# Two-layer decoder step on one core: prompt attention's denominators spread by matmuls from their columns, and the row turns of the q, k, v projections behind the next part's first tile

## The chip, the cores and the metric

The kernel runs on one core of one Trainium2 chip. The metric is the device time of one execution in microseconds (us). The engines are TensorE (PE; its weight loads are listed as PEld), VectorE (DVE), ScalarE (ACT), GpSimd (POOL) and SyncE (SP), whose queue issues nearly all of this kernel's DMAs. Each works through its own instructions in order and waits for the others by semaphores.

## What is computed

The reference is one inference step of a decoder trunk of two layers over 512 prompt tokens and 8 sample tokens (each with a past of 4096), model width 1024. The kernel holds both kinds as columns 0 to 519 of one transposed activation (samples first). Cut to what matters here:

```python
# layer 0: multi-head latent attention, 16 heads; prompt part
s = (q_nope @ k_nope + q_pe @ k_pe) * scale          # per head, causal
p = softmax(s)                                        # rows of 128 queries
o = p @ v                                             # then @ w_o, residual, MLP
# layer 1: dilated attention, 3 groups (window, dilation) = (128,1), (512,4), (2048,16), 8 heads of 64
qkv = (x @ w_qkv).reshape(B, S, 3, 3, 8, 64)          # q, k, v of each group
# prompt: per group scores, exp, values; merged by denominators
# sample: keys and values of the stored state plus the new k, v
# returned too: for each group the last rows of k and v (prompt) and the updated state (sample)
# then @ w_o, residual, MLP, final norm
```

Every output of the reference is stored: the two activations, the latents, and the k and v rows of the dilated groups.

## The kernel before

All large matrix products are made by `linear` and `whole`: a weight chunk of 8 x 128 rows by 256 columns (1 MB) is loaded by SyncE into one of two slots (`chunk`), ScalarE rounds it into a high part (L1936), GpSimd subtracts to get the low part (L2281), and TensorE makes three products for each 128 x 128 weight tile and each half of 260 columns (L529, L530, L533). One output tile of 128 rows by 520 columns takes 48 matmuls into one of four PSUM units of two banks each; `z_begin` lets TensorE write a unit when all but the last three units before it have been taken (`tile_taken`), and `z_end` counts `tile_summed`. SyncE may load chunk n when the split of chunk n-2 is done (`chunk_low`).

**Prompt attention** goes over 16 heads in pairs and four query tiles of 128 for each pair: step n is pair p = n // 4, tile t = n % 4. TensorE's step holds, in this order: `scores(n)` (L738), at t = 2 `values(p-1)` (L779) and `spread_den(p-1)` (L767), `turn(n-2, 0)` (L753), one projection of the next pair for t < 3 (`project`, L529 to L533 for q, L706 to L708 for k), at t = 3 `latent_queries` (L718), `turn(n-2, 1)`, and at t = 1 `turn_den(p-1)` (L760). The turns are transposes of the exponentials, one per key block, into PSUM bank 4 or 5; ScalarE copies them out (`keep`, L2044 and L2047). The list `turn_order` numbers everything that goes through banks 4 and 5, and all waits on `turned_ready` and `turned_taken` are counted by it. VectorE masks the scores and takes their maximum (L1546 to L1548), ScalarE exponentiates and sums (`probs`, L2031).

The division by the softmax denominators is put off to the output. VectorE takes the reciprocals of eight columns (L1551: two heads by four query tiles). `turn_den` turns them to eight rows, ScalarE copies these (`rdenT`, L2078), `spread_den` multiplies them with a table `pick8` into bank 4, so that each half of 64 rows holds the reciprocals of its head over 512 columns, ScalarE copies that (`shareP`, L2067), and VectorE multiplies the output with it (L1561). The output goes on to ScalarE (`hA`, L2083) and GpSimd. The last pair has no projection beside it (n < 28 only), nor do the steps behind it.

**The q, k, v projections of layer 1** go over nine parts `QKV` (q of the three groups, then k, then v), each with four output tiles in two weight chunks; tiles are numbered 0 to 35. VectorE takes each tile with a multiplication (L1775) into `dq`, `dk` or, for v, the scratch `tmp` (and copies the samples' columns into `vS`, L1778). At the end of a part TensorE waits until all its tiles are taken and turns them to rows by `to_rows` (L936, four transposes a unit): one unit for the eight samples, one more per kept tile of k (one for group 0, four for groups 1 and 2), four for v. VectorE copies a unit out (`row_tile`, L1690), k and samples into `nat`, a buffer of two slots, each free again when its store has landed (`nat_stored`), v into `dv`. SyncE's `store_part` waits for each row unit and stores it (L1238); for part p-1 it stands behind both chunks of part p in SyncE's queue.

Spread over the same tiles is the attention of the samples (`sample_step`): behind tiles 8 to 11, 13 to 16 and 18 to 21 VectorE scores two of the 24 (group, sample) key blocks each, a product (L1705) and a sum (L1707) for each; their keys (`load_keys`, L1271) and queries (`load_queries`, L1279, the stored q rows spread to 128 partitions) are loaded by SyncE. Behind tiles 24 to 28 come new scores (L948; VectorE L1718 to L1733), maxima and sums (L955, L959, L963), and behind tiles 28, 30, 32, 34 the values of two samples each (L972), whose value rows SyncE loads by `load_values` (L1286) into eight buffers; L980 behind tiles 29, 31, 33, 35 sums them. In SyncE's queue the first eight value loads stand at part 7 behind `store_part` of part 6; loads 14 to 19 and 20 to 23 follow the two chunks of the output projection, which stand behind `store_part` of part 7.

## Time and profile before

| what | value |
|---|---|
| three runs | 1597.49, 1596.48, 1589.59 us; median 1596.48 |
| profiled execution | 1591.77 us, its span 1589.9 us |
| mean granted TensorE clock | 0.970 of 2.4 GHz |
| TensorE's matmuls | busy 1471.6 us, 93% of the span |
| prompt attention | 102 to 262 us |
| q, k, v projections | 850 to 1091 us |
| ScalarE copy and GpSimd split of a weight chunk | L1936 1486 ns and L2281 3541 ns, means over 127 |
| ScalarE exponential (L2031) | 525 ns mean over 64 |
| value and key rows from the state, 256 KB | 5.8 us median from issue to landing |

The profile is of one execution. A row of the chain gives the start, the length, the engine, the tile or line, and how many instructions it merges; a row of a timeline adds the operation, the shapes, and in square brackets how long the engine had been idle before it and what ended that. Matmuls of 32-bit operands leave two records each. The page's clock line for 40 slices of 39.7 us reads 9969996999899999999999999999979999999999, in tenths of full speed.

### The profile page before, as it was taken

To read this page: it belongs to the slowest core of one execution; us is meant where nothing else is said; L and a number is where in the kernel's file an instruction comes from. 1 tells how busy PE (TensorE), PEld (TensorE's weight loads), DVE (VectorE), ACT (ScalarE), POOL (GpSimd) and SP (SyncE) were. 2 spreads that over 40 slices of the span, in tenths; PEclk is the share of its full clock that TensorE was granted. 3 is DMA by queue.
4 is the path that set the end of the run, shared out by engine and by line. 5 is a ranking of instruction groups with operands and counts; after the bars stand their busy time and mean duration, and the time that the engine had idled before them with its cause. 6 is when DMAs were issued, how large, how long until landed. Compare 5 with 4: busy or idle time off the path is not lost.

```text
span 1589.9 us, 28142 instructions
## 1 busy us (share of the span) xinstructions
PE 1471.6 (93%) x12047; PEld 1356.4 (85%) x12047; DVE 686.2 (43%) x984; ACT 470.2 (30%) x882; POOL 613.0 (39%) x276
## 2 busy tenths in 40 slices
PE   6969996788999999999999999998879999999997
PEld 6857763455799999999999999887669999999997
DVE  4667775787245410143113456324567330034212
ACT  4215554333332211122321111113633221122222
POOL 2412222343245644466343434222014654356441
PEclk9969996999899999999999999999979999999999
DMA  4234753776234543453433465556932543533421
GB/s 156 75 100 160 245 183 121 274 295 239 87 134 159 185 159 132 139 202 137 158 140 124 135 233 186 168 198 212 324 126 71 195 150 141 209 135 132 159 80 54
DMA packets 124075, 258.80 MB, mean 163 GB/s; under 512 B 7265, under 2 KB 104689, under 8 KB 117713
## 3 DMA queue, kind: packets, MB, share of 16 engines
q1 hardware_dynamic: 117840, 219.75, 40.1%
q0 software_dynamic: 6144, 37.75, 6.4%
q8 instruction: 68, 1.11, 0.3%
q14 instruction: 23, 0.18, 0.0%
HBM read 249.88 MB, written 95.58 MB: 217 GB/s over the span
## 4 chain that ended last, share of the span: by engine, by line
PE 83%; DVE 9%; issue 3%; ACT 2%; DMA 2%; SPq 1%; another core or an unknown queue 0%; POOL 0%; DVEq 0%; ACTq 0%
PE ps L529 22%; PE ps L533 22%; PE ps L530 21%; PE ps L830 4%; PE ps L738 2%; PE ps L851 1%; ACT sc L2229 1%; PE ps L779 1%; PE ps L753 1%; DVE KT L1536 1%; PE ps L1021 1%; PE ps L1055 1%; DVE sq L1705 1%; PE ps L718 1%; PE ps L871 1%
## 5 line engine op out<-in xcount | busy, mean ns | idle before, releaser
L2281 POOL TENSOR_TENSOR whl<-wraw,whl 128x2048 fp32r<-128x2048 f32 (+3 forms) x127 | 448.6, 3541 | 554.6 <-ACT whl L1936 554.6
L529 PE MATMUL ps<-hA,whl 128*128 128x260 f32 x1216 | 323.2, 287 | 11.6 <-POOL hA L2281 6.0
L530 PE MATMUL ps<-hA,whl 128*128 128x260 f32 x1216 | 318.4, 283 | 0.0
L1936 ACT ACTIVATE whl<-wraw 128x2048 fp32r<-128x2048 f32 (+3 forms) x127 | 186.1, 1486 | 437.3 <-PE ps L533 379.4
L529 PE MATMUL ps<-uT,whl 128*128 128x260 f32 x1024 | 268.4, 283 | 0.0
L530 PE MATMUL ps<-uT,whl 128*128 128x260 f32 x1024 | 266.3, 281 | 0.0
L533 PE MATMUL ps<-hA,whl 128*128 128x260 f32 x1216 | 247.2, 285 | 0.0
L529 PEld LDWEIGHTS ps<-hA,whl 128*128 128x128 f32 x1216 | 231.1, 190 | 16.6 <-issue 15.2
L530 PEld LDWEIGHTS ps<-hA,whl 128*128 128x128 f32 x1216 | 231.8, 191 | 0.1
L533 PE MATMUL ps<-uT,whl 128*128 128x260 f32 x1024 | 206.8, 283 | 0.0
L530 PEld LDWEIGHTS ps<-uT,whl 128*128 128x128 f32 x1024 | 193.2, 189 | 0.0
L529 PEld LDWEIGHTS ps<-uT,whl 128*128 128x128 f32 x1024 | 192.6, 188 | 0.0
L533 PEld LDWEIGHTS ps<-hA,whl 128*128 128x128 f32 x1216 | 187.9, 190 | 0.0
L1649 DVE TENSOR_TENSOR xT<-xT,ps 128x520 f32<-128x520 f32 (+1 forms) x48 | 33.4, 696 | 351.9 <-PE ps L533 341.2
L529 PE MATMUL ps<-hB,whl 128*128 128x260 f32 x640 | 168.3, 284 | 0.0
L530 PE MATMUL ps<-hB,whl 128*128 128x260 f32 x640 | 166.8, 282 | 0.0
L533 PEld LDWEIGHTS ps<-uT,whl 128*128 128x128 f32 x1024 | 156.7, 188 | 0.0
L2281 POOL TENSOR_TENSOR uT<-tmp,uT 128x520 f32 x64 | 84.3, 1318 | 132.2 <-ACT uT L1946 132.2
L1668 DVE SCALAR_TENSOR_TENSOR tmp<-ps,rstd 128x520 f32<-128x520 f32 x64 | 44.8, 700 | 200.3 <-PE ps L533 199.7
L533 PE MATMUL ps<-hB,whl 128*128 128x260 f32 x640 | 129.0, 283 | 0.0
L530 PEld LDWEIGHTS ps<-hB,whl 128*128 128x128 f32 x640 | 120.7, 189 | 0.1
L529 PEld LDWEIGHTS ps<-hB,whl 128*128 128x128 f32 x640 | 120.4, 188 | 0.1
(299 smaller groups left out, 2019.5 us busy)
## 6 DMA issues: line engine op xcount, KB each, us to landing
out_ds<-in_state SPq DMA_DIRECT2D x32, 2047.0 KB, 10.2
wraw<-in_w_up SPq DMA_DIRECT2D x32, 1024.0 KB, 5.6
wraw<-in_w_down SPq DMA_DIRECT2D x32, 1024.0 KB, 5.1
wraw<-in_w_qkv SPq DMA_DIRECT2D x18, 1024.0 KB, 5.6
out_ds<-in_state SPq DMA_DIRECT2D x8, 2044.0 KB, 12.5
dv<-in_state SPq DMA_DIRECT2D x36, 256.0 KB, 5.8
dv<-q_scratch SPq DMA_DIRECT2D x6, 1024.0 KB, 7.2
wraw<-in_w_omla SPq DMA_DIRECT2D x4, 1024.0 KB, 12.3
```

What stands on the lines that cost most here:

```text
L529: pe.matmul(ps[:, 2 * u + a, 0:HALF], hi(k), rhs(k, 0)[:, c], start=first, stop=False)
L530: pe.matmul(ps[:, 2 * u + a, 0:HALF], hi(k), rhs(k, 1)[:, c], start=False, stop=False)
L533: ins = pe.matmul(ps[:, 2 * u + a, 0:HALF], lo(k), rhs(k, 0)[:, c], start=False, stop=last)
L718: ins = pe.matmul(ps[:, 6 + k, LQ + h * NS:LQ + (h + 1) * NS], wuk_pair(p)[:, a, k * P:(k + 1) * P], qS[0:NOPE, h, :], start=True, stop=Tr ...
L738: ins = pe.matmul(ps[:, 2 * (n % 2) + a, 0:(t + 1) * P], qh[:, h % 4, tok], kh[:, h % 4, 0:(t + 1) * P], start=True, stop=True)
L753: ins = pe.transpose(ps[:, bank, b * P:(b + 1) * P], pr[:, n % 3, a, b * P:(b + 1) * P], ident[:])
L779: ins = pe.matmul(ps[a * VD:(a + 1) * VD, 5, b * P:], v[:, b, h * VD:(h + 1) * VD], turned(a, b, 1, slice(b * P, NP)), start=(b == 0), sto ...
L830: ins = pe.matmul(ps[64 * g:64 * g + 64, k, 0:UC], qbd[b % 2][:, j, :, :].rearrange("p q h -> p (q h)"), moving, start=(j == 0), stop=(j = ...
L1649: free(dve.tensor_tensor(cols(xT, f), cols(xT, f), zt(u), ALU.add))
L1668: free(dve.scalar_tensor_tensor(out=out, in0=zt(u), scalar=0.0, in1=rooted(u), op0=ALU.max, op1=ALU.mult))
L1936: ins = act.activation(dst(0), src, ACT.Copy)
L2281: return pool.tensor_tensor(dst, src, hi.bitcast(F32), ALU.subtract)
```

## The change

**Denominators.** `turn_den`, `rdenT` and `pick8` are gone. `spread_den` takes the column of reciprocals itself as weights, repeated over 64 weight columns, with the identity as the moving operand: eight matmuls (four query tiles by two heads, each into its half of 64 rows) in place of four. The exponentials of a pair's first tile (t = 0, one block a head) are turned by `turn_first` for both heads at once into bank 4, behind the projection of the same step, and copied by one instruction (`keep_first`) behind the second head's exponentials. All other turns stay.

**Row turns.** `part_rows(p-1)` stands behind the first tile of part p and its sample step, on TensorE and VectorE; the rows of the last part stay where they were. The first tile of part 7 goes to the end of `dv` for group 1 in place of `tmp`, which is still to be read. On SyncE `store_part` of part p-2 stands behind the first chunk of part p (from part 3 on), that of part 0 behind chunk 4 together with the first two query loads and four key loads, and those of parts 7 and 8 behind the value loads that follow the two chunks of the output projection. The first eight value loads so stand behind the store of part 5 and chunk 15.

```diff
@@ -413,12 +410,14 @@
                 if n % NB_T == 2 and 6 <= n:
                     order.append(("share", n // NB_T - 1, 0))
                 if 2 <= n < NI + 2:
-                    order += [("probs", n - 2, 0), ("probs", n - 2, 1)]
-                if n % NB_T == 1 and n >= 5:
-                    order.append(("den", n // NB_T - 1, 0))
+                    order += [("probs", n - 2, a) for a in range(2 if (n - 2) % NB_T else 1)]
             return order
 
         TURN = {item: i for i, item in enumerate(turn_order())}
+
+        def turned_at(n, a):
+
+            return TURN["probs", n, a if n % NB_T else 0]
 
         def turn_bank(item):
 
...
@@ -448,6 +447,17 @@
         def strip(i, gi):
 
             return slice(32 * (2 * i + gi % 2), 32 * (2 * i + gi % 2) + 32)
+
+        def rows_of(p_):
+
+            gi, part_ = QKV[p_]
+            return 1 + (len(kept_tiles(gi)) if part_ == 1 else NB_T if part_ == 2 else 0)
+
+        def v_tile(p_, f):
+
+            if p_ == 7 and f == 0:
+                return dv[:, 1, :, :].rearrange("p t c -> p (t c)")[:, NB_T * GH * E - T:].rearrange("p (o n) -> p o n", o=1)
+            return tmp[:, f:f + 1, :]
 
         def due(count):
 
...
@@ -753,24 +763,30 @@
                     ins = pe.transpose(ps[:, bank, b * P:(b + 1) * P], pr[:, n % 3, a, b * P:(b + 1) * P], ident[:])
                 ins.then_inc(turned_ready, 1)
 
-            def turn_den(p):
+            def turn_first(n):
+
+                pe.wait_ge(probs_ready, 2 * n + 2)
+                earlier = turn_earlier(("probs", n, 0))
+                if earlier is not None:
+                    pe.wait_ge(turned_taken, earlier + 1)
+                for a in range(2):
+                    ins = pe.transpose(ps[:, 4, a * P:(a + 1) * P], pr[:, n % 3, a, 0:P], ident[:])
+                ins.then_inc(turned_ready, 1)
+
+            def spread_den(p):
 
                 pe.wait_ge(reciprocal_ready, p + 1)
-                pe.wait_ge(turned_taken, turn_earlier(("den", p, 0)) + 1)
-                pe.transpose(ps[0:8, 4, 0:P], rdens[:], ident[:]).then_inc(turned_ready, 1)
-
-            def spread_den(p):
-
-                pe.wait_ge(share_table_in, 16)
                 pe.wait_ge(turned_taken, turn_earlier(("share", p, 0)) + 1)
                 for t in range(NB_T):
-                    ins = pe.matmul(ps[:, 4, t * P:(t + 1) * P], pick8[:, t * P:(t + 1) * P], rdenT[:], start=True, stop=True,
-                                    skip_group_check=True)
+                    for a in range(2):
+                        ins = pe.matmul(ps[a * VD:(a + 1) * VD, 4, t * P:(t + 1) * P],
+                                        rdens[:, 2 * t + a:2 * t + a + 1].to_broadcast([P, VD]), ident[:],
+                                        start=True, stop=True, skip_group_check=True)
                 ins.then_inc(turned_ready, 1)
 
             def values(p):
 
-                pe.wait_ge(turned_taken, TURN["probs", NB_T * p + NB_T - 1, 1] + 1)
+                pe.wait_ge(turned_taken, turned_at(NB_T * p + NB_T - 1, 1) + 1)
                 if p:
                     pe.wait_ge(output_taken, p)
                 for b in range(NB_T):
...
@@ -796,21 +812,21 @@
                 if t == 2 and p:
                     values(p - 1)
                     spread_den(p - 1)
-                if 2 <= n < NI + 2:
+                if 2 <= n < NI + 2 and t != 2:
                     turn(n - 2, 0)
                 if t < 3 and n < NI - NB_T:
                     project(t)
                     if t == 2 and p == H // 2 - 2:
                         mark["projected"] = vw.at("tile_summed")
+                if 2 <= n < NI + 2 and t == 2:
+                    turn_first(n - 2)
                 if t == 3 and n < NI - NB_T:
                     pe.wait_ge(tile_taken, vw.at("tile_summed"))
                     latent_queries(p + 1)
                 if n == NI - 1:
                     new_scores()
-                if 2 <= n < NI + 2:
+                if 2 <= n < NI + 2 and t != 2:
                     turn(n - 2, 1)
-                if t == 1 and p:
-                    turn_den(p - 1)
 
             pe.wait_ge(tile_taken, vw.at("tile_summed"))
 
...
@@ -981,19 +997,33 @@
                                         start=True, stop=True, skip_group_check=True)
                     z_end(ins)
 
+            part_summed = []
+
+            def part_rows(p_):
+
+                gi, part_ = QKV[p_]
+                pe.wait_ge(tile_taken, part_summed[p_])
+                src = (dq, dk, None)[part_]
+                def get(f, c):
+                    return v_tile(p_, f)[:, 0, c] if src is None else src[:, gi, f, c]
+                to_rows(lambda f: get(f, slice(0, NS)), NS, gi)
+                for t in (kept_tiles(gi) if part_ == 1 else range(NB_T) if part_ == 2 else []):
+                    to_rows(lambda f: get(f, far(t) if part_ == 2 and gi else slice(NS + t * P, NS + (t + 1) * P)), P, gi)
+
+            def after_tile(tile):
+
+                sample_step(tile)
+                if tile and tile % 4 == 0:
+                    part_rows(tile // 4 - 1)
+
             for p_, (gi, part_) in enumerate(QKV):
                 for c in range(2):
                     if p_ == c == 0:
                         first_linear(hA_k, DT - 1)
                     else:
-                        linear(KC, 2, MC, hA_k, lambda mt: sample_step(4 * p_ + 2 * c + mt))
-                pe.wait_ge(tile_taken, vw.at("tile_summed"))
-                src = (dq, dk, None)[part_]
-                def get(f, c):
-                    return tmp[:, f, c] if src is None else src[:, gi, f, c]
-                to_rows(lambda f: get(f, slice(0, NS)), NS, gi)
-                for t in (kept_tiles(gi) if part_ == 1 else range(NB_T) if part_ == 2 else []):
-                    to_rows(lambda f: get(f, far(t) if part_ == 2 and gi else slice(NS + t * P, NS + (t + 1) * P)), P, gi)
+                        linear(KC, 2, MC, hA_k, lambda mt: after_tile(4 * p_ + 2 * c + mt))
+                part_summed.append(vw.at("tile_summed"))
+            part_rows(8)
             pe.wait_ge(tile_taken, vw.at("tile_summed"))
 
             def d_scores(k):
...
@@ -1296,20 +1325,21 @@
                 for c in range(2):
                     i = 2 * p + c
                     chunk((0, (KC, MC), wsrc(io["w_qkv"], 0, KC, (3 * gi + part_) * ce + c * MC, MC)))
+                    if i == 4:
+                        sp.wait_ge(tile_taken, mark["ffn0"])
+                        store_part(*QKV[0])
+                        load_queries(0)
+                        load_queries(1)
+                        keys_until(4)
                     if i >= 7:
                         keys_until(4 + used_by(2 * (i - 3) + 1))
                     if i in (8, 9, 10, 11):
                         load_queries(i - 6)
+                    if c == 0 and p >= 3:
+                        store_part(*QKV[p - 2])
                 if p == 8:
                     for n in range(8, 14):
                         load_values(n)
-                if p:
-                    store_part(*QKV[p - 1])
-                if p == 1:
-                    sp.wait_ge(tile_taken, mark["ffn0"])
-                    load_queries(0)
-                    load_queries(1)
-                    keys_until(4)
                 if p == 7:
                     sp.wait_ge(keys_summed, 3 * NS)
                     for n in range(8):
...
@@ -1318,7 +1348,7 @@
                 chunk((0, (4, 2 * MC), wsrc(io["w_odil"], 0, 4, c * 2 * MC, 2 * MC)))
                 for n in ((14, 15, 16, 17, 18, 19), (20, 21, 22, 23))[c]:
                     load_values(n)
-            store_part(*QKV[8])
+                store_part(*QKV[7 + c])
             for s_ in range(2):
                 sp.wait_ge(nat_stored[s_], NATS[s_] * 16)
             copy_some(10)
...
@@ -1767,16 +1797,9 @@
                     u = z_take()
                     free(dve.tensor_copy(mine[:, :, 2 * q:2 * q + 2], ps[:, 2 * u, 0:8].rearrange("p (f i) -> p f i", f=4)))
 
-            for p_, (gi, part_) in enumerate(QKV):
-                for f in range(4):
-                    u = z_take()
-                    out = cols(tmp, f) if part_ == 2 else (dq, dk)[part_][:, gi, f:f + 1, :].rearrange(
-                        "p f (a b) -> p f a b", a=2)
-                    free(dve.tensor_tensor(out, zt(u), rooted(u), ALU.mult))
-                    if part_ == 2:
-                        dve.wait_ge(tile_taken, vw.at("tile_summed"))
-                        dve.tensor_copy(vS[:, gi, f, :], tmp[:, f, 0:NS])
-                    sample_step(4 * p_ + f)
+            def part_rows(p_, nn):
+
+                gi, part_ = QKV[p_]
                 if due(16 * (nn // 2)):
                     dve.wait_ge(nat_stored[nn % 2], 16 * (nn // 2))
                 row_tile(NS, nat[0:NS, nn % 2, :])
...
@@ -1787,9 +1810,25 @@
                     nn += 1
                 for t in (range(NB_T) if part_ == 2 else []):
                     row_tile(P, dv[:, gi, t, :])
+                return nn
+
+            for p_, (gi, part_) in enumerate(QKV):
+                for f in range(4):
+                    u = z_take()
+                    out = (v_tile(p_, f) if part_ == 2 else (dq, dk)[part_][:, gi, f:f + 1, :]).rearrange(
+                        "p f (a b) -> p f a b", a=2)
+                    free(dve.tensor_tensor(out, zt(u), rooted(u), ALU.mult))
+                    if part_ == 2:
+                        dve.wait_ge(tile_taken, vw.at("tile_summed"))
+                        dve.tensor_copy(vS[:, gi, f, :], v_tile(p_, f)[:, 0, 0:NS])
+                    sample_step(4 * p_ + f)
+                    if p_ and f == 0:
+                        nn = part_rows(p_ - 1, nn)
                 if p_ == 5:
+                    dve.wait_ge(tile_taken, vw.at("tile_summed"))
                     dve.tensor_tensor(prodS[:], dq[:, :, :, 0:NS], dk[:, :, :, 0:NS], ALU.mult).then_inc(products_ready, 1)
 
+            nn = part_rows(8, nn)
             a0 = vw.at("a")
             for s_ in range(2):
                 dve.wait_ge(nat_stored[s_], NATS[s_] * 16)
...
@@ -2027,10 +2066,19 @@
                 p, t = n // NB_T, n % NB_T
                 act.wait_ge(max_ready, n + 1)
                 if n >= 3:
-                    act.wait_ge(turned_ready, TURN["probs", n - 3, a] + 1)
+                    act.wait_ge(turned_ready, turned_at(n - 3, a) + 1)
                 act.activation(pr[:, n % 3, a, 0:(t + 1) * P], ps[:, 2 * (n % 2) + a, 0:(t + 1) * P], ACT.Exp,
                                bias=nbs[:, 2 * (n % 2) + a:2 * (n % 2) + a + 1], scale=MLA_SCALE,
                                accum_out=dens[:, p % 2, 2 * t + a:2 * t + a + 1]).then_inc(probs_ready, 1)
+
+            def keep_first(n):
+
+                p = n // NB_T
+                taken(("probs", n, 0))
+                if p:
+                    act.wait_ge(output_ready, p)
+                act.activation(wt[:, :, 0, WC // 2:WC // 2 + P], ps[:, 4, 0:2 * P].rearrange("p (a c) -> p a c", a=2),
+                               ACT.Copy).then_inc(turned_taken, 1)
 
             def keep(n, a):
 
...
@@ -2065,17 +2112,17 @@
                     if p >= 2:
                         act.wait_ge(output_taken, p - 1)
                     act.activation(shareP[:], ps[:, 4, :], ACT.Copy).then_inc(turned_taken, 1)
-                if 2 <= n < NI + 2:
+                if 2 <= n < NI + 2 and t != 2:
                     keep(n - 2, 0)
                 if 1 <= n <= NI:
                     probs(n - 1, 1)
                 if 2 <= n < NI + 2:
-                    keep(n - 2, 1)
+                    if t == 2:
+                        keep_first(n - 2)
+                    else:
+                        keep(n - 2, 1)
                 if NI - 2 <= n < NI + 2:
                     copy_queries(n - (NI - 2))
-                if t == 1 and p:
-                    taken(("den", p - 1, 0))
-                    act.activation(rdenT[:], ps[0:8, 4, 0:P], ACT.Copy).then_inc(turned_taken, 1)
                 if t == 2 and p:
                     act.wait_ge(output_taken, p)
                     n_ = vw.n.get("a", 0) % 4
...
```

## Rows read from the trace of the kernel before

**Rows 1.** The page, chain of work that ended last: shares by engine
```profile
PE 83%; DVE 9%; issue 3%; ACT 2%; DMA 2%; SPq 1%; another core or an unknown queue 0%; POOL 0%; DVEq 0%; ACTq 0%
```

**Rows 2.** TensorE's waits, 102 to 262 us: in total, times, longest
```profile
PE ps L753 <- ACT shareP L2067: 5.5, 7, 0.8
PE ps L738 <- ACT pr L2031: 2.2, 6, 1.2
```

**Rows 3.** TensorE's waits, 839 to 1092 us
```profile
PE ps L936 <- DVE dq L1775: 2.4, 3, 0.8
```

**Rows 4.** The chain in order of time, one head pair: start, length, what
```profile
187.76 2.30 PE ps L779 x16
190.07 1.10 PE ps L767 x8
191.19 0.61 ACT shareP L2067
...
191.93 0.30 PE ps L753
...
193.66 0.11 PE ps L753
...
205.10 0.11 PE ps L760
...
206.50 2.30 PE ps L779 x16
```

**Rows 5.** The chain in the dilated attention, 1124 to 1132 us
```profile
1129.48 1.41 PE ps L1055 x16
```

**Rows 6.** VectorE's timeline, 845 to 1092 us: start, length, line, operation
```profile
868.33 0.70 DVE L1775 TENSOR_TENSOR dq<-ps,rstd 128x520 f32<-128x520 f32 x1 [5.07 <-PE ps L533]
...
874.09 0.70 DVE L1775 TENSOR_TENSOR dq<-ps,rstd 128x520 f32<-128x520 f32 x1 [5.06 <-PE ps L533]
...
926.16 4.38 DVE L1705 TENSOR_TENSOR sq<-dv 128x512 f32<-128x512 f32 x1
...
959.36 0.70 DVE L1775 TENSOR_TENSOR dk<-ps,rstd 128x520 f32<-128x520 f32 x1
...
970.07 0.70 DVE L1775 TENSOR_TENSOR dk<-ps,rstd 128x520 f32<-128x520 f32 x1 [1.83 <-PE ps L533]
...
987.35 0.70 DVE L1775 TENSOR_TENSOR dk<-ps,rstd 128x520 f32<-128x520 f32 x1 [1.72 <-PE ps L533]
...
996.27 0.70 DVE L1775 TENSOR_TENSOR tmp<-ps,rstd 128x520 f32<-128x520 f32 x1 [1.09 <-PE ps L533]
...
999.09 0.28 DVE L1733 TENSOR_TENSOR mS<-mS,sN 128x64 f32<-128x64 f32 x1
...
1014.66 0.70 DVE L1775 TENSOR_TENSOR tmp<-ps,rstd 128x520 f32<-128x520 f32 x1 [4.18 <-PE ps L533]
...
1023.57 0.70 DVE L1775 TENSOR_TENSOR tmp<-ps,rstd 128x520 f32<-128x520 f32 x1 [4.38 <-PE ps L533]
...
1035.82 0.70 DVE L1775 TENSOR_TENSOR tmp<-ps,rstd 128x520 f32<-128x520 f32 x1 [5.16 <-PE ps L533]
...
1042.45 0.70 DVE L1775 TENSOR_TENSOR tmp<-ps,rstd 128x520 f32<-128x520 f32 x1 [5.65 <-PE ps L533]
...
1050.24 0.70 DVE L1775 TENSOR_TENSOR tmp<-ps,rstd 128x520 f32<-128x520 f32 x1 [5.25 <-PE ps L533]
...
1059.61 0.70 DVE L1775 TENSOR_TENSOR tmp<-ps,rstd 128x520 f32<-128x520 f32 x1 [4.56 <-PE ps L533]
...
1071.50 0.70 DVE L1775 TENSOR_TENSOR tmp<-ps,rstd 128x520 f32<-128x520 f32 x1 [5.27 <-PE ps L533]
```

**Rows 7.** SyncE's timeline, 838 to 1115 us
```profile
1019.68 3.31 SPq L1286 DMA_DIRECT2D dv<-in_state  x4
```

**Rows 8.** The chain, 1056 to 1092 us
```profile
1056.67 6.39 DMA sq<-in_state
```

**Rows 9.** Stretch 240 to 260: TensorE, VectorE, ScalarE, GpSimd; clock, DMA, GB/s
```profile
240.00:260.00 20.00, 16.89 (x63) 9.44 (x63) 9.63 (x25) 11.24 (x34) 1.26 (x1) 0.65 0.09 37
```

20 lines of the change are left out of this document (7 added, 13 removed).

## The prediction

> **What bounds the kernel now.** I read the chain of work that ended last first: TensorE holds 83% of it [rows 1], so an edit is worth what it takes out of TensorE's own sequence, idle time included, where TensorE is what ends last. Then I read TensorE's waits in the two stretches that the change touches (prompt attention, 102 to 262 us; the q, k, v projections of the second layer, 850 to 1091 us), the chain inside one attention period, and VectorE's timeline in the projections, whose takes of the tiles (L1775) mark when TensorE ended each tile.
>
> In attention one head pair takes 18.7 us (L779 starts at 187.76 and again at 206.50 on the chain [rows 4]). TensorE is idle once in it on ScalarE: it waits for the copy of the spread denominators before it may write bank 4 again, 5.5 us in seven waits [rows 2]. In the projections a tile costs 5.76 us (874.09 less 868.33) [rows 6]; what a pair of takes shows above that is row turns, waits and sample work.
>
> **Part 1, denominators.** Per period, on TensorE, out of the chain [rows 4]:
> - Removed: the turn of the reciprocals (L760), 0.11. ScalarE's copy of it (L2078) and the small table load go too; both lie beside other work, so nothing.
> - The wait: the spread (L767) ends at 191.17, ScalarE copies it in 0.61, L753 starts at 191.93: 0.76. Now the third projection (from 192.23, where L753 ends, to 193.66: 1.43) stands there and covers it. The cover is needed: without it (the last two head pairs have no projection) the wait stays.
> - Row turns of the first tile: 0.30 after the wait plus 0.11 at 193.66 become two in one place, 2 x 0.11 = 0.22, so 0.19 less. They need ScalarE's copy of the spread, ready some 0.8 us before the projection ends.
> - Added: the spread is eight matmuls of 64 weight columns by 128 for four of 128 by 128. Before has 1.10 for eight records [rows 4], 0.137 each; sixteen at that price are 2.20. The nearest row is that of the dilated values (L1055, 64 weight columns, 128 moving): 16 records in 1.41 [rows 5]. The lower end is 1.0, four pairs side by side without the hand-over between records. I take 1.36, near the 16-record row, the same number in the same pairs and here without a stretch's start: +0.26, between -0.1 and +1.1.
>
> Sum per period: -0.11 -0.76 -0.19 +0.26 = -0.80. What is late next: scores of tile 3 need ScalarE's exponentials of tile 1. ScalarE copies the spread (0.61), then makes them in some 0.6 (0.53 on the page's mean, and hand-over), 1.3 behind the spread's end; TensorE asks at 1.43+0.22 = 1.65. The projection's VectorE chain and the max chain only shift along. It holds in six periods: 6 x 0.80, 4.9 us unrounded. For the last two I take 0.
>
> The Trainium skill, "TensorEngine Tiling (Array Packing)", Performance Considerations and Key Properties, says that column-tiled halves of 64 run in parallel; by it the spread would stay at 1.10 and the sum gain another 1.6 us. The 16-record row of this case, 0.088 a record against 0.137 for the full-width spread, is only part of the way there.
>
> **Part 2, row turns.** Before, at the end of each of nine parts TensorE waits until VectorE has taken the fourth tile, 0.8 each [rows 3], then turns the rows; now it goes on with the next part's first tile and turns the rows behind it. VectorE's order moves likewise: take of the first tile, its sample work, then the row copies. TensorE may be three PSUM units ahead of VectorE.
> - Parts 0 to 2 (q, one row unit): -0.8 each, -2.4. Part 3 (k of group 0, two units): -0.8.
> - Part 4 (five units, now behind tile 20). Before: 970.07 less 959.36 less 5.76 = 4.95 over the tile [rows 6]. Now the fifth unit waits until VectorE has taken tile 20 (0.7), scored two samples (four operations of about 0.65 to 0.7, the two of L1705 and the two of L1707) and copied the first row (0.7): about 4.6, then its own 0.6: 5.2. +0.25.
> - Part 5 (behind tile 24). Before: 996.27 less 987.35 less 5.76 = 3.16, and 0.4 for the new scores. VectorE's sample work behind this take reaches 999.37, 3.1 after it, then a row copy of 0.7; the fifth unit starts near 3.85 and the tile follows at 4.45. Against 3.56: +0.9.
> - Part 6 (behind tile 28). Before, two tiles: 3.15 and 1035.82 less 1023.57 less 5.76 = 6.49, together 9.64. An unstalled values step costs 1050.24 less 1042.45 less 5.76 = 2.03, so some 4 of the 6.49 is the wait for the value rows from HBM. Why they are late: SyncE issues them (L1286) at 1019.68, behind the stores of part 6's rows [rows 7], and a value load takes up to 6.39 from issue to landing [rows 8]. Now those stores come after, and the eight loads stand behind part 5's stores, whose last row is copied some 9.5 us after tile 24, while they are needed 28 us after it: about 10 us to spare. Then tile 28 has 0.3 (a sum) + 2.03 + five turns of about 0.5 = 4.8. -4.8.
> - Part 7 (behind tile 32). Before: 3.61 and 6.13, 9.74, with the same wait (the load issued at 1056.67) [rows 6, 8]. Now the loads for tile 32 are issued when tile 30's values are taken, some 3 us after that tile, and no longer behind part 7's stores; they are needed at 14.4, spare 4. Tile 32 then has the earlier 0.79 of sample sums, 2.03 and 2.5 of turns: 5.35. -4.4.
> - Part 8: as before, 0.
>
> The queue that is moved past: SyncE. The second weight chunk of a part now stands behind the stores of the part before last. It is asked for two tiles or more ahead: chunk 13 is issued about 10 us behind tile 20's end, lands 6 to 8 later and is wanted by ScalarE at 22.5, so nothing; chunk 5, behind 3 MB of query and key loads, is the tightest, with some 4 us. The last four value loads now stand behind part 7's stores and a chunk: landed at about 14, needed at 16.9.
>
> Sum of part 2: -2.4 -0.8 +0.25 +0.9 -4.8 -4.4 = -11.3. Both: -16.2.
>
> **Against which time.** The profiled execution took 1591.77 (span 1589.9, 1.9 around it): 1575.6. The median of the three others is 4.7 above it: 1580.3. The four executions have a mean of 1593.8; from it 1577.6, my number. Some 0.5%, 8 us, is what a measurement of this kernel can tell from no change.
>
> **Rivals.**
> A. Value loads are still late. Both stalls, about 4.1 each, need the loads in time; the last four loads could add a third. For it: one took 6.39 to land [rows 8], and a chunk shares the queue. Against: 3 to 10 us to spare. If both stalls stay: -16.2 +8.2 = -8.0, 1585.8. Chance 0.12.
> B. VectorE falls behind at the moved row copies. Its products of two SBUF tiles stretch when GpSimd splits a chunk: one took 4.38 in place of 0.68 [rows 6]. If such a one falls between the take and the row copies behind tiles 16, 20 and 24 or delays the take, TensorE waits 3.7 each: -16.2 +7.4 for two, 1585.0. Against: GpSimd starts its split when ScalarE's copy of the chunk is done, right behind a chunk's last tile, and needs some 5; the moved rows stand behind a chunk's first tile, 5.76 later, where it is nearly done. The Trainium skill, "SBUF — State Buffer", says that a VectorE instruction with two SBUF inputs and a GpSimd one that reads SBUF exclude each other; the trace agrees (4.38). Chance 0.12.
> C. The change doesn't do what it says in attention: TensorE's saved idle is given back at the next VectorE chain or at ScalarE's exponentials. For it: TensorE already waits 2.2 us in six for exponentials [rows 2]. Then -11.3: 1582.5. Chance 0.10.
> D. Slower. The granted clock: it was 0.65 at 240 to 260 us [rows 9], a mix of 1.2 and 2.4 GHz, behind steps in which TensorE waited on both other engines, while the steady periods before ran at 2.4 (the page's clock line shows 9 there). Should the regrouped step bring the 1.2 GHz level into the steady periods, the matmuls of a period, some 17 of its 18.7 us, would take twice as long; from one whole period on that eats the 16.2, and two give 1577.6 + 34 = 1611.6. Against: the change takes idle time out. Chance 0.04.
> E. The opposite: the half-clock stretch behind 246 us shrinks, since the last steps close up. 16.89 us of matmuls at 0.65 would be some 6 shorter at full clock [rows 9]: 1571.6. Chance 0.10.
>
> **How the numbers follow.** Forecast 0.52, A 0.12, B 0.12, C 0.10, E 0.10, D 0.04. Range: down to E with the parallel spread and the slowest-to-fastest half spread of the runs (1571.6 -1.6 -2 = 1568); up to A with about 3 for the runs, 1589. That leaves out D and combinations of A and B. Faster by over 0.5%: forecast, C, E and most of A and B, 0.85; within 0.5%: 0.10; slower: 0.05.
>
> **What would show it.** Right: L753 no longer waits on L2067 in the six periods, which take 17.9; the spread's 16 records take 1.3 to 1.4; no wait of L936 on L1775; tile 28 to 29 and 32 to 33 about 10.6 apart; no wait of L972 on a load. The forecast is wrong if the fifth row unit waits far longer than 4.6, if VectorE's L1705 operations of 4 us sit right before row copies, or if the chunk copies of ScalarE wait for their DMA and TensorE for them.

## The result and the profile after

The changed kernel takes 1571.09 us, median of 4 runs (1568.32 to 1573.06), against 1596.99 of the kernel before (4 runs, 1589.59 to 1597.57): a ratio of 0.983, 95% interval 0.981 to 0.986. The forecast was 1577.6 with a range of 1568 to 1589. The profiled execution took 1569.71, with a span of 1567.9, 22.0 less than the span before. The gain that was forecast was 16.2; by these medians it is 25.9, by the two profiled executions 22.

Line numbers have moved: the turns of the probabilities are L763 (L753 before) and, for a pair's first tile, L773; scores L748 (L738); spread L782 (L767); values L795 (L779); row turns L952 (L936); takes L1820 (L1775); row copies L1720 (L1690); the sample sums L988 (L972); value loads L1315 (L1286).

The page's chain of work that ended last, by engine, answers to [rows 1]: TensorE's share is up from 83%.

```profile
PE 86%; DVE 8%; issue 2%; ACT 2%; another core or an unknown queue 0%; DMA 0%; SPq 0%; POOL 0%; DVEq 0%; ACTq 0%
```

The chain of one head pair of the changed kernel (start, length, what), to be laid beside [rows 4]:

```profile
147.22 2.31 PE ps L795 x16
149.53 0.87 PE ps L782 x16
150.40 0.31 PE ps L716
150.71 0.12 PE ps L717
...
151.88 0.12 PE ps L718
152.00 0.22 PE ps L773 x2
152.22 1.72 PE ps L748 x4
...
163.55 1.29 PE ps L748 x4
164.84 2.19 PE ps L795 x13
```

The period is 164.84 less 147.22, 17.62, for 18.73 before: 1.11 less. ScalarE's copy has left the chain, the spread takes 0.87 in place of 1.10, and the turn of the reciprocals is gone. The projection starts right behind the spread, but its first matmul takes 0.31 where it took 0.12 behind L753: the first record behind the spread takes some 0.2 longer, whichever it is. A record of a turn that follows the projection takes 0.11 in both kernels, so this is no price of every change of kind. Five periods give 5.55 (values at 131.60 and 225.21 before, 129.63 and 217.69 after) and the sixth another 1.11.

TensorE's waits, 820 to 1066 us, in total, times and longest. They answer to [rows 3]:

```profile
PE ps L952 <- DVE nat L1720: 4.4, 2, 2.8
PE ps L952 <- DVE mine L1798: 0.3, 1, 0.3
```

In this stretch no wait on a take and none of L988 on a load is left; there is a new one, on the copies of rows. VectorE's takes, whose distances are the tiles' (tiles 20, 21, 24, 25, 28, 29, 32, 33; compare [rows 6]):

```profile
949.82 0.70 DVE L1820 TENSOR_TENSOR dk<-ps,rstd 128x520 f32<-128x520 f32 x1 [2.42 <-PE ps L543]
962.35 0.70 DVE L1820 TENSOR_TENSOR dk<-ps,rstd 128x520 f32<-128x520 f32 x1 [3.10 <-PE ps L543]
...
979.63 0.70 DVE L1820 TENSOR_TENSOR tmp<-ps,rstd 128x520 f32<-128x520 f32 x1 [4.77 <-PE ps L543]
990.00 0.70 DVE L1820 TENSOR_TENSOR tmp<-ps,rstd 128x520 f32<-128x520 f32 x1 [0.42 <-PE ps L543]
...
1007.96 0.70 DVE L1820 TENSOR_TENSOR dv<-ps,rstd 128x520 f32<-128x520 f32 x1 [4.47 <-PE ps L543]
1018.27 0.70 DVE L1820 TENSOR_TENSOR tmp<-ps,rstd 128x520 f32<-128x520 f32 x1 [4.32 <-PE ps L543]
...
1039.32 0.70 DVE L1820 TENSOR_TENSOR tmp<-ps,rstd 128x520 f32<-128x520 f32 x1 [5.65 <-PE ps L543]
1049.40 0.70 DVE L1820 TENSOR_TENSOR tmp<-ps,rstd 128x520 f32<-128x520 f32 x1 [4.56 <-PE ps L543]
```

Tile 20 to 21 takes 12.53, by far the longest distance; 24 to 25, 28 to 29 and 32 to 33 take 10.37, 10.31 and 10.08. VectorE behind tile 20, and TensorE's row turn that waits for it (the number in brackets is the idle time before it):

```profile
953.03 0.69 DVE L1737 TENSOR_REDUCE sS<-sq 128x8 f32<-128x512 f32 x1
953.63 1.27 DVE L1720 COPY nat<-ps 8x512 f32<-8x512 f32 x2
...
954.36 1.05 PE L952 MATMUL ps<-ident,dk 128*128 128x128 f32 x4 [2.82 <-DVE nat L1720]
```

SyncE's value loads for tile 28 are issued 17.5 ahead of its take, before it was 3.9 (1023.57 less 1019.68 [rows 6, 7]):

```profile
990.47 2.54 SPq L1315 DMA_DIRECT2D dv<-in_state  x4
```

The last two head pairs. First two lines of the chain, the four score products of tile 31 before and after; then the stretch of 20 us of the changed kernel (columns as in [rows 9]: busy times, clock, DMA, GB/s):

```profile
246.39 3.78 PE ps L738 x4
```

```profile
236.85 1.95 PE ps L748 x4
```

```profile
230.00:250.00 20.00, 15.06 (x85) 8.35 (x85) 10.95 (x30) 11.95 (x35) 1.27 (x2) 0.86 0.18 72
```

The same four products take 1.95 in place of 3.78, and the granted clock of the stretch is 0.86 in place of 0.65: much less of it runs at 1.2 GHz. (Taken from 231.40, which lies to the last pairs as 240 did before, it is 0.83.)

From stage to stage along the two chains, the 22.0 of the profiled executions divide so: -2.0 ahead of the first head pair's values, where nothing was changed; -6.7 in six periods; -3.9 from the last pair's values to the first key turn (241.10 to 264.21 before, 232.47 to 251.66 after); +1.0 between there and the second layer; -10.6 in the projections; +0.1 behind them.

### The profile page after: what moved, and what is told of

It reads as the page before. It is cut to its first block, busy times and chain, and to the rows that moved or that the text cites. A ratio compares the mean times of both kernels' runs of the same rounds, so it can differ in the third digit from the quotient of the medians.

```text
span 1567.9 us, 28214 instructions
## 1 busy us (share of the span) xinstructions
PE 1461.7 (93%) x12103; PEld 1354.0 (86%) x12103; DVE 673.4 (43%) x984; ACT 467.1 (30%) x866; POOL 612.9 (39%) x276
## 4 chain that ended last, share of the span: by engine, by line
PE 86%; DVE 8%; issue 2%; ACT 2%; another core or an unknown queue 0%; DMA 0%; SPq 0%; POOL 0%; DVEq 0%; ACTq 0%
PE ps L539 23%; PE ps L543 23%; PE ps L540 22%; PE ps L846 4%; PE ps L748 2%; PE ps L867 1%; ACT sc L2276 1%; DVE KT L1566 1%; PE ps L795 1%; PE ps L1051 1%; PE ps L763 1%; PE ps L1085 1%; PE ps L952 1%; PE ps L887 1%; PE ps L728 1%
```

## The experiments

Each time is a median; the kernel before, measured along with each group of four, had 1595.81 (13 runs, 1589.4 to 1601.9), 1595.47 (18 runs, 1589.3 to 1601.5) and 1596.53 (17 runs, 1590.5 to 1602.5).

**The halves apart, and the rows ahead of the samples.** The changed kernel again:

> The changed kernel again, beside the others. The two profiled executions differ by 22.0 us (1589.9 to 1567.9 spans), the medians by 25.9. Theory 1 (the profiled execution of before was a fast one): the difference of the medians comes out at 24 to 27 again, and its trace shows the same 17.6 us per head pair and about 230 us from the first to the last tile taken. Rival (the medians were luck): 20 to 23.

1572.93 (1572.27 to 1575.33, 6 runs), ratio 0.986 (0.983 to 0.989). The difference of the medians is now 22.9, in the rival's range and not in the theory's. Its profiled execution was the slowest of the six, 1575.33. In it the sixth period is not shorter than before (15.89): it takes 16.08, with a granted clock of 0.79 between 228 and 236 us.

```profile
219.26 2.31 PE ps L795 x16
...
235.34 2.30 PE ps L795 x16
```

Only the denominators (part 1):

> Only the first part of the change: the denominators spread from their columns, and the first tile's turns behind the projection. The row turns of the projections stay as in before. Theory 1 (the two parts add up, read from where the two traces drift apart: 11.5 us by the end of prompt and sample attention): 10 to 14 us faster than before. Rival (only the steady periods are real, 6 x 1.1, and the rest of the drift is the clock's phase, which another execution loses): 6 to 8 us faster.

1584.9 (1576.32 to 1592.34, 8 runs), ratio 0.993 (0.990 to 0.996). Only the rows, with SyncE's order (part 2):

> Only the second part: row turns behind the next part's first tile and SyncE's queue in the new order. Theory 1 (adds up): the stretch from the first tile's take to the dilated scores is 10.6 us shorter, as between the two traces, and so is the time: 10 to 12 us faster than before. Rival (the two parts share a gain, such as the same run-to-run swing of the clock): 12 to 16 us faster.

1583.63 (1582.72 to 1583.89, 6 runs), ratio 0.9925 (0.990 to 0.995). So 10.9 and 12.2 off the kernel before, together 23.1 where both make 22.9: the halves add up. The second half seems to do something more: its 6 runs lie within 1.2 of each other, the 8 of the first half within 16, the 13 of the kernel before within 12. That overstates it: measured again (below), six of its runs lie within 4.9. Over all groups the runs of a kernel with the new order lie within 1.2 to 10.1 (4 to 7 runs each), those with the old order within 9.4 to 16 (8 to 18 runs each). The chain in the projections of the denominators-only kernel, whose SyncE order is that of before, shows one way in which a run gets long:

```profile
905.91 9.04 DMA dv<-q_scratch
914.98 4.14 DVE sq L1709
...
920.83 5.65 DMA dv<-q_scratch
926.51 4.11 DVE sq L1709
...
937.05 9.13 DMA dv<-q_scratch
946.21 1.25 DVE sq L1709
...
951.33 4.95 DVE sq L1709
956.90 0.68 DVE nat L1694
```

The queries land late, VectorE's products of two SBUF tiles start late and stretch from 0.68 to over 4, and the row copy that TensorE needs comes last: "PE ps L941 <- DVE nat L1694: 5.6, 1, 5.6". The last of the stretched products, right ahead of that copy, runs beside a GpSimd split of 4.50 that starts at 951.22. From tile 19 to tile 20 it is 16.74 here and 10.71 before; the projection stage takes 259.3 in this profile and 250.4 in the profile before.

The changed kernel with the rows of a part ahead of the sample work, on TensorE and on VectorE:

```
                 def after_tile(tile):
-                    sample_step(tile)
                     if tile and tile % 4 == 0:
                         part_rows(tile // 4 - 1)
+                    sample_step(tile)
... (VectorE's loop likewise)
```

> The changed kernel with the moved row turns placed ahead of the sample step of the same tile, on TensorE and VectorE. Theory 1 (behind tiles 20 and 24 the fifth row unit waits for VectorE's sample work, 2.8 and 1.6 us, and the first of these waits also costs a drop of the granted clock to 1.2 GHz): tile 20 to 21 takes about 8.7 in place of 12.5, tile 24 to 25 about 9.2 in place of 10.4, the granted clock stays at 1.00 at 950 to 960 us, and the kernel is 4 to 6 us faster than the changed one. Rival (VectorE's wait for the stores of nat blocks the sample work, and that the next tile): 0 to 2 us faster, with VectorE's take of tile 21 or 22 late.

1564.7 (1560.11 to 1569.42, 6 runs), 8.2 less than the changed kernel beside it, where the theory had 4 to 6. In a second measurement (below) it has 1565.28.

**SyncE's order alone.** The stores and loads in the changed order, every engine as before; the heart of the edit:

```
+                    if i == 4:
+                        sp.wait_ge(tile_taken, mark["ffn0"])
+                        store_part(*QKV[0])
+                        load_queries(0)
+                        load_queries(1)
+                        keys_until(4)
...
+                    if c == 0 and p >= 3:
+                        store_part(*QKV[p - 2])
...
-                if p:
-                    store_part(*QKV[p - 1])
```

> Only the order of SyncE's queue in the projections is the changed kernel's: the first part's rows are stored and the first queries and keys loaded behind the fifth chunk, each later part's rows are stored behind the first chunk of the next but one. Every engine does what it did before, so the row turns still stand at the ends of their parts. Theory (the queue order carries the gain of the second part): the two waits for value rows, about 4.1 each, go, because their loads no longer stand behind the stores of the part just ended; tiles 28 to 29 and 32 to 33 shrink by some 4 each; and the runs lie within 2 of each other where those of the kernel before lie within 12, because the query loads are no longer late. About 8 to 11 faster than before, 1585 to 1588. Rival (the place of the row turns carries it, the loads were hidden): within 3 of before, with the same spread of runs.

1583.59 (1579.2 to 1584.88, 7 runs), 11.9 off. That is the whole of what part 2 brought (12.2). The runs lie within 5.7, not within 2 as the theory had it. TensorE's waits in its projections (830 to 1092 us):

```profile
PE ps L936 <- DVE dq L1776: 2.4, 3, 0.8
PE ps L936 <- DVE dk L1776: 2.4, 3, 0.8
```

The waits on the takes are all there, as in [rows 3], but none on a load. The takes of tiles 28 and 29:

```profile
1022.79 0.70 DVE L1776 TENSOR_TENSOR tmp<-ps,rstd 128x520 f32<-128x520 f32 x1 [4.39 <-PE ps L533]
1030.76 0.70 DVE L1776 TENSOR_TENSOR tmp<-ps,rstd 128x520 f32<-128x520 f32 x1 [4.97 <-PE ps L533]
```

7.97 for 12.25 before [rows 6]: 4.3 of stall gone; for tiles 32 and 33 it is 7.79 for 11.89.

**The value loads alone.** The kernel before, with the first eight value loads ahead of part 6's stores and the last ten ahead of part 7's; queries and keys as before:

```
-                if p:
+                if p == 7:
+                    sp.wait_ge(keys_summed, 3 * NS)
+                    for n in range(8):
+                        load_values(n)
+                if p and p < 8:
                     store_part(*QKV[p - 1])
```

> Only the value loads are moved on SyncE: the first eight ahead of the stores of part 6 and not behind them, the last ten ahead of the stores of part 7; all else is the kernel before, the query loads and the row turns too. Theory (the two stalls were value loads behind stores): about 8 faster than before, 1586 to 1589, with tiles 28 to 29 and 32 to 33 about 4 shorter each, but the runs still differ by some 10, since the query loads are where they were. Rival (the stall moves to another wait, as the rows turned or the stores that now come later): 0 to 3 faster.

1587.33 (1579.61 to 1593.01, 12 runs): 8.1 off, and the runs still 13 apart, both as the theory has it. Of the 12 that SyncE's order is worth, 8 are the value loads; the other 4, and the narrower spread, belong to what else it moves. That these are the query loads is argued, from profiles such as that of the denominators-only kernel: no run moves the query loads alone. Here too TensorE waits for a row copy behind stretched products, in an execution at the median of its kernel (1587.63), and tile 19 to tile 20 takes 16.38:

```profile
PE ps L936 <- DVE nat L1690: 4.9, 1, 4.9
```

**The two halves of the denominators**, each on top of the changed projections and measured in another group than the rows-only kernel (1583.63, and 1583.05 when measured again). First the spread of the reciprocals' columns without the turn and the copy:

```
-                    ins = pe.matmul(ps[:, 4, t * P:(t + 1) * P], pick8[:, t * P:(t + 1) * P], rdenT[:], start=True, stop=True,
-                                    skip_group_check=True)
+                    for a in range(2):
+                        ins = pe.matmul(ps[a * VD:(a + 1) * VD, 4, t * P:(t + 1) * P],
+                                        rdens[:, 2 * t + a:2 * t + a + 1].to_broadcast([P, VD]), ident[:],
+                                        start=True, stop=True, skip_group_check=True)
```

> The projections as changed, and of the denominators only the direct spread: eight products of the reciprocals' columns, no turn of the reciprocals, no copy of it. The row turns of tile 0 stay where they were, so TensorE still waits for ScalarE's copy of the spread before it turns them. Theory: per head pair 0.11 less for the turn and 0.2 less for the spread itself, the wait of 0.76 stays; eight pairs, 2 to 3 faster than the kernel with only the projections changed (1583.6), so 1580.5 to 1582, and the stretch of the last two pairs (39.0 with the old denominators, 34.0 with the new) stays near 38. Rival (turning the reciprocals, with its wait for their VectorE chain, was what delayed the last pairs): that stretch falls to about 34 here, and the time to 1576 or 1577.

1576.59 (1573.88 to 1580.89, 6 runs), 7.0 off the rows-only kernel, where the theory had 2 to 3. A head pair takes 18.40 for 18.72, the 0.3 expected; but the end of attention (from the last-but-one pair's values to the first key turn, the sixth period in it) takes 35.0 for 39.0. Both numbers are near those of the rival. Then the moved turns without the new spread:

```
-                if 2 <= n < NI + 2:
+                if 2 <= n < NI + 2 and t != 2:
                     turn(n - 2, 0)
...
+                if 2 <= n < NI + 2 and t == 2:
+                    turn_first(n - 2)
```

> The projections as changed, and of the denominators only the other half: the two row turns of tile 0 are put together behind the third projection, with one copy of both; the reciprocals are still turned and spread through the table. Theory: the wait for the copy of the spread (0.76) and 0.19 of turns go in six pairs, 5 to 6 faster than the kernel with only the projections changed (1583.6), 1577.5 to 1579; a head pair takes about 17.8. The last two pairs stay near 39.0. Rival (these turns shape the last pairs): that stretch falls to 34 or 35 here, and the time to 1573.

1571.47 (1569.16 to 1579.27, 6 runs), 12.2 off the rows-only kernel and as fast as the kernel with both edits (1571.09 and 1572.93): what the new spread adds to the moved turns is seen in the length of a period and not in the total. Five periods of 0.76 and the last pairs' 4.5 (the sixth is in them) are 8.3 of the 12.2; the rest is in no stage that was touched. A head pair takes 17.96, 0.76 less; the last pairs 34.5. So in these profiles either edit alone takes 4 to 4.5 out of the last pairs, and both together 5.0, and they say through what: the granted clock. One profile each overstates how well this is known. The old attention has 39.0 in three profiles (before, before again, rows only) and 37.6 to 37.7 in four (the other kernels with it), the new one 33.7 to 34.0 in three and 35.3 in two, so the gain of both edits is 2.3 to 5.3. Three stretches of 20 us there, of the kernels rows-only, new spread and moved turns:

```profile
240.00:260.00 20.00, 16.91 (x64) 9.46 (x65) 9.50 (x24) 10.69 (x31) 1.26 (x1) 0.63 0.06 23
```

```profile
238.00:258.00 20.00, 14.72 (x96) 8.21 (x95) 10.42 (x26) 10.78 (x31) 2.22 (x2) 0.91 0.07 29
```

```profile
237.00:257.00 20.00, 15.58 (x80) 8.91 (x79) 10.94 (x27) 11.01 (x31) 2.53 (x3) 0.83 0.05 20
```

The rival of the new spread's run, that turning the reciprocals, with its wait for VectorE, was what delayed the last pairs, falls as the whole cause with the second kernel: it still has that turn, and that wait of 0.7, and gains as much.

**Second looks.** The kernel before again:

> The kernel before, unchanged, with a second profile. Theory (its runs differ because the first loads of queries, behind the first parts' stores on SyncE, land now early, now late, beside the weight chunks): a run near the median of 1595.5 or above shows a projection stage longer than the 250.4 of the first profile, 253 to 260, with VectorE's products of queries and keys late and TensorE waiting 3 to 6 on the copy of a row; a run near 1590 looks like the first profile. Rival (the clock alone makes the difference): the projection stage is 250.4 again and the difference lies in stretches with a granted clock under 1, in the last two head pairs and the dilated attention.

1594.72 (1591.03 to 1600.42, 8 runs). Its profiled execution was one of 1592.86; the projections took 250.0, as in the first profile, and the dilated attention behind them 4.0 more than there. It tells nothing of a long run's queries, and speaks for the clock as one source of the swing. So does the mean clock of each run: of the 17 runs in its group the three above 1600 all had 0.965, the fastest two 0.970 and 0.973. But the clock is not all of it. Of the 18 runs in the second group, eight had a mean clock of 0.970 or 0.971: four of them took 1589.3 to 1590.3, four 1596.2 to 1597.3. Some 7 at one clock is near the 5.7 to 6.0 that the late copies cost between tiles 19 and 20 above. That a run of this very kernel has them stays unseen.

SyncE's order and the whole of part 2, side by side:

> The kernel before with the changed kernel's SyncE order alone, a second time and now beside the kernel with the whole second part, on one chip. Theory (the place of the row turns is worth the 2.0 that the profiles of the projection stage differ by, 242.0 against 240.0): 1 to 3 slower than the next kernel. Rival (the turns' place is worth nothing to the whole, as the two medians of 1583.6 say): within 1 of it.

> The whole second part without the first, a second time: row turns behind the next part's first tile and SyncE's order with them. Theory: 1582 to 1583.9, 1 to 3 faster than the kernel with SyncE's order alone. Rival: within 1 of that kernel; what the stage gains is then given back behind it, in the dilated attention, where the granted clock dips two or three times.

1581.42 (1579.15 to 1584.89, 6 runs) against 1583.05 (1579.87 to 1584.79, 6 runs). The profiles again have the projection stage shorter with the row turns moved, by 2.5 (239.8 for 242.3) where it was 2.0 in the first pair (240.0 for 242.0), and the whole is not shorter: the means of all runs are 1582.4 (13 runs) and 1583.0 (12). The rival holds for the total. Where the 2 of the stage go, the profiles don't say: the named place, the dilated attention, took 76.8 and 73.3 with the turns moved, 74.1 and 73.3 without. The mean granted clock of all these runs was 0.967 with the turns moved (12 runs) and 0.970 without (13), so the kernel with the turns moved spends more of its time at 1.2 GHz; how much of the 2 that takes was not measured.

The rows ahead of the samples, again:

> The changed kernel with the rows of a part turned and copied straight behind the next part's first tile, and the sample work of that tile behind them, a second time. Theory (VectorE's row copies no longer stand behind its sample work, so TensorE's wait of 2.8 and 1.6 on them is gone, and the granted clock does not fall behind it): 1562 to 1567, some 5 to 9 faster than the changed kernel. Rival (the first measurement was a lucky set of clock dips): 1569 to 1572.

1565.28 (1562.18 to 1567.59, 5 runs), ratio to before 0.980 (0.978 to 0.982). The projections take 235.3 in both its profiles, for 239.8 of the changed kernel. VectorE behind tile 20:

```profile
951.33 0.70 DVE L1820 TENSOR_TENSOR dk<-ps,rstd 128x520 f32<-128x520 f32 x1 [2.42 <-PE ps L543]
951.95 1.26 DVE L1720 COPY nat<-ps 8x512 f32<-8x512 f32 x2
```

The copies follow the take at once, and the waits of 4.4 on them are down to one of 0.9. The granted clock is 1.00 there:

```profile
955.00:957.00 2.00, 2.00 (x19) 2.00 (x19) 0.81 (x2) 0.00 (x0) 0.00 (x0) 1.00 0.41 158
```

So the sample work in front of the row copies costs the changed kernel 4.5 in this stage. The whole is 8.2 shorter in the group that holds both; by the means of all runs 7.9 (1564.6 of 11 runs, 1572.5 of 10). What goes beyond the stage's 4.5 is not placed. This is the fastest kernel of the study.

## Why the prediction was right, and where its steps were not

**Part 1, the period.** Forecast -0.80, measured -1.11. (The terms as printed give 4.8 for six periods, not 4.9; nothing hangs on it.) The wait of 0.76 and the turn of 0.11 went as said, and in these periods the copy was never late. Two terms were mis-sized. The spread was put at +0.26 and came at -0.23 (0.87 for 1.10): sixteen records of 64 columns (eight products) are faster than eight records of 128 (four products), not slower; the range's lower end of -0.1 was too high, and the row of the dilated values, 0.088 a record [rows 5], was a poor neighbour, since 0.87 is 0.054 a record. The Trainium skill, "TensorEngine Tiling (Array Packing)", Key Properties, says that different tiles can load weights and multiply in parallel. The forecast went only part of the way with it; its estimate by that page was a spread that stays at 1.10, and with 0.87 the trace is nearer to that than to the 1.36 taken from the row. The other term was the 0.19 for the row turns: the 0.30 of L753 was not the turn's price but that of the first record behind the spread, and the projection now pays it (0.31). With the moved turns behind the old spread it pays it too (0.32), and with the new spread alone the turn does (0.30). Apart, the two edits gave 0.33 and 0.76, which is the 1.11 but for 0.02.

**The last two pairs.** Forecast 0, as no projection covers the wait there. Behind the six periods they gained 3.9 all the same, which is rival E, given 0.10, with 6 from the stretch in [rows 9]. Its mechanism was right, seen in the granted clock, 0.86 for 0.65. Its size was two thirds by this pair of profiles and less by others: the same stretch, from the last pair's values to the first key turn, takes 21.7 to 21.8 in four profiles with the old attention, 2.5 more than the 19.2 of the changed kernel, and 23.1 in three. This and the spread put the profiled result below the forecast. What decides whether the stretch falls to 1.2 GHz was not settled; either of two different edits keeps more of it at full clock.

**Part 2.** Along the takes, against the forecast: parts 0 to 3 -3.8 (-3.2); part 4 +1.8 (+0.25); part 5 +1.0 (+0.9); part 6 -5.1 (-4.8); part 7 -4.6 (-4.4); in all -10.6 (-11.3). The two stalls went by the mechanism named, the loads behind the stores, and rival A (late all the same) did not come. The step of part 2 that failed is part 4's, and not at the wait: TensorE's fifth unit was forecast 4.6 behind the take of tile 20 and starts 4.54 behind it (954.36). But behind that wait of 2.82 the granted clock falls to the 1.2 GHz level in the projections, which the forecast had weighed for attention alone (rival D). The same wait and a fall behind it are in all six profiles with this order of the rows, and in neither of the two with the rows ahead of the samples, so the order brings it. The unit takes 1.05 in place of 0.6, and tile 21 starts at half clock: its first matmuls take 0.22 on the chain and not 0.12. The granted clock from there on, in steps of 2 us:

```profile
955.40:957.40 2.00, 2.00 (x12) 2.00 (x11) 1.13 (x2) 0.00 (x0) 0.00 (x0) 0.50 0.36 138
957.40:959.40 2.00, 2.00 (x17) 2.00 (x16) 0.94 (x2) 0.00 (x0) 0.00 (x0) 0.88 0.66 255
959.40:961.40 2.00, 2.00 (x19) 2.00 (x18) 0.00 (x0) 0.00 (x0) 0.00 (x0) 1.00 0.60 167
```

Tile 21 takes 6.95 from 955.40 to its take, 1.19 more than 5.76; with 0.45 of the unit this is the missing 1.6. Behind tile 24 the same wait is 1.6 long, and no clock is lost (4.6 over the tile; the forecast had 4.45). A wait of 2.5 for value rows in the kernel before lost none either (granted clock 1.00 from 1060 to 1072 us); what decides it is open.

**What part 2 is made of.** The forecast gave the row turns 3 of the 11.3 and SyncE's order 8.2. The runs give SyncE's order 12 to 15 and the place of the turns nothing in the total. The 8.2 of the value loads was right (8.1). What the forecast missed is the other 4 or more that the old order costs; that this is query loads landing late in some runs is the likely cause, not a shown one. The forecast read one profile in which they cost TensorE nothing, and took that profile's stage for the usual one.

**Against which time.** From the profiled execution the forecast was 1575.6, and 1569.7 came. By medians the gain was 23 to 26, by the first pair of profiles 22 (of which 2.0 lie ahead of all edits), by the second profile of the changed kernel 16.4 against the same profile of before. The forecast gain of 16.2 was too small by 7 to 10 of the medians; the forecast time is only 6.5 off because it was counted from a mean of four, 1593.8, that lies 1.7 to 3.2 below the medians of the kernel before. That the time came out so near is in part luck. Rival B (VectorE held up by its stretched products) did not come in the changed kernel (none of the 24 products takes over 1.27), and C (attention gives its saving back) did not either: the five steady periods are shorter in both profiles, and the two halves add up. D (1.2 GHz in the steady periods) did not come in the first profile. In the second the sixth period had it for a part and lost its gain by it, 16.08 for 14.78, far from D's doubled periods.

## What to carry to other kernels

A load that stands behind a store on the same queue is issued, as here, when that store's producer is done, not when the load could go (3.9 ahead of its tile's take before, 17.5 after): read where each queue's next loads stand before moving compute, since here the order of one queue was worth all that the second half brought. Work moved off a stall must also be put ahead of the helper work on the engine that takes its result, or it waits there. And where the same kernel's runs differ by more than a few tenths of a per cent, take more than one profile before reading a stage's length as its usual one.

## What the runs showed of the hardware

Eight fp32 products (sixteen records) with 64 weight columns and 128 moving ones, in pairs for the two column halves, took 0.87 in the changed kernel and 0.90 in the one with the new spread alone, for 1.10 of four products (eight records) of full width. Their weights are one column read 64 times over; no run has the same products with 64 columns of their own, so whether that costs anything is not shown.

The granted clock differs between runs of one kernel. Three stretches of the dilated attention of the changed kernel, and the same three of its second profile, in which that part took 76.8 in place of 73.2 (columns as before; the clock is the third number from the end):

```profile
1102.61:1110.61 8.00, 6.78 (x56) 5.41 (x58) 4.61 (x12) 5.37 (x19) 0.00 (x0) 0.79 0.95 321
1118.61:1126.61 8.00, 5.77 (x58) 4.01 (x56) 5.32 (x13) 6.57 (x23) 0.00 (x0) 1.00 0.88 297
1134.61:1142.61 8.00, 4.79 (x105) 3.22 (x109) 3.04 (x8) 6.31 (x21) 0.00 (x0) 1.00 1.10 377
```

```profile
1104.75:1112.75 8.00, 6.77 (x54) 5.57 (x56) 4.65 (x12) 5.67 (x20) 0.00 (x0) 0.79 1.08 338
1120.75:1128.75 8.00, 5.86 (x46) 4.03 (x42) 5.39 (x13) 5.18 (x18) 0.00 (x0) 0.79 1.02 330
1136.75:1144.75 8.00, 5.13 (x76) 3.33 (x73) 4.49 (x9) 5.60 (x20) 0.00 (x0) 0.79 1.04 340
```
